# A hybrid attention and MLP layer in which the differential heads' outputs and probabilities are turned by VectorE and DRAM in place of TensorE, and their scores come one weight piece later

## The chip, the cores and the metric

One core of one Trainium2 chip runs the whole program. The metric is the device time of one execution in microseconds, the median of the runs. TensorE, VectorE, ScalarE, GpSimd and SyncE (called PE, DVE, ACT, POOL and SP in the profile) each run their own stream of instructions in order and meet at semaphores; SP issues nearly all DMAs.

## The reference, cut to what matters

The input is 256 tokens of width 2048, float32. One layer is a mixer with eight FoX heads and eight differential heads, an output projection, and a gated MLP with a causal convolution of width 3.

```python
h = rms_norm(x, norm1_g)
proj = h @ w_in                               # 2048 x 6152: q, k, v of 16 heads, 8 forget logits
# FoX head: p_f = softmax(q k' * scale + c_q - c_k, causal);  o_f = p_f @ v
#   c = cumsum(log_sigmoid(forget logits)), so every FoX head needs a row and a column of c
# differential head: two 64-wide softmaxes over a block-causal mask
a_d = p_d[:, :, 0] - lam * p_d[:, :, 1]
o_d = rms_norm(a_d @ v, diff_subln_g) * (1 - lambda_init)
x = x + concat(o_f, o_d) @ w_out
x = x + (silu(conv(h2 @ w_up)[gate]) * conv(h2 @ w_up)[val]) @ w_down
```

## The kernel before, in words

All weights are read once from DRAM in pieces of 128 partitions, by a ring of four slots (`raw`, line 305). Each piece is split into a high part (ACT, line 697, `w_hi`) and a low part (DVE, line 1138, `w_lo`), and PE multiplies it in three float32r passes. PE's order is written out by hand: the program is a row of pieces, and small attention steps are put between them.

The input projection is cut by heads into "frames" of eight pieces. Differential heads are frames 0 to 7 and their attention is numbered 1 to 8; FoX heads follow, numbered 9 to 16. While PE projects head f (counting from 0; 12 matmuls of 384 columns a piece), the other engines do the attention of head f, whose projection was frame f-1, and the end ("trail") of head f-1. Within a frame, slot b means "beside or behind piece b". On every engine the slot's own work stands in program order with the split of the piece four further on: ACT's split in slot b waits until piece b is used, and SP's load in slot b waits for DVE's split of slot b.

Before the change a differential frame goes so. PE: values of head f-1 (lines 446 to 448, which read `pT`) and transposes of q and k (line 410) after piece 2, scores (line 419, which read `qkT`) after piece 3, transposes of the output (line 465) after piece 4. ACT: `copy_p`, the copy of the turned probabilities from `p_read` to `pT` (line 774), in slot 0; `copy_qkT` (lines 737, 738) in slot 2; exponentials (line 757) in slot 3; in slot 7 the evacuation (lines 719, 722) and the guess of the norm first and the split after. DVE: row maxima (1224) and normalisation (1254) ahead of the splits of slots 3 and 4, the norm of the output (1279) in slot 2, the low part of `mixed` (1289) ahead of the split of slot 6. POOL rotates q and k (1693, 1696) once DVE has normed them, and PE's transposes wait for that.

From head 4 on the probabilities are turned without PE: DVE transposes blocks of 32x32 (`turn_p`, line 1265), SP stores them to a scratch in DRAM (line 314) in slot 3 and reads them back block by block in four DMAs (line 324) in slot 5. FoX heads from 10 on do the same in slots 6 and 7, and PE reads `p_read` itself (lines 457, 458) after piece 5 of the next frame. Heads 1 to 3, 15 and 16 use PE transposes (line 428).

In slot 6 of frame 6 SP issues `cbc` (line 355), a broadcast of all c rows to 128 partitions, and `cq` (line 356), the columns of c, an access of single elements of 4 bytes. SP's next load, slot 7 of frame 6, brings piece 7 of frame 7, which ACT splits in slot 3 of frame 7. None of this is edited by the change.

Of the kernel before, what the change touches and what calls it, by code (L numbers as in the profile page):

```python
# [13 lines left out]
P = 128  # L14
S, D, F = 256, 2048, 5504
H = 8
# [55 lines left out]
P0, P_STOP = 4, HEADS - 1  # L72
BLOCK_AT = dict(scores=5)
MOVES = {1: (0, 5), 2: (5, 16)}
DIFF_AT = dict(turn=2, scores=3)
TRAIL_AT = dict(values=2, sums=2, norm=2, turn=4, hi=5, lo=6)
CONV_TAIL = {11 + 3 * t: (FULL - 1, t, BATCH) for t in range(BATCH)} | {28 + 3 * t: (FULL, t, LAST) for t in range(LAST)}
FORGET_AT = dict(scale=0, logits=0, exp=1, log=2, turn=3)
OUT_AT = dict(turn=1, scores=2, probs=4, values=5)


def hybrid_layer_kernel(nc, xT_d, xtok_d, w0_d, win_d, wrest_d, const_d, row_d, vec_d, out_d):
    c_d = nc.dram_tensor("c_scratch", (H, S), F32, kind="Internal").ap()
    p_d = nc.dram_tensor("p_scratch", (P, SROW), F32, kind="Internal").ap()
    with ExitStack() as ctx:
# [22 lines left out]
        with ExitStack() as att:  # L108
# [40 lines left out]
            on = sa("on", S)  # L149
# [40 lines left out]
        osq_done, oturn_done, ors_done, onorm_done = sem("osq_done"), sem("oturn_done"), sem("ors_done"), sem("onorm_done")  # L190
# [48 lines left out]
        def part(t, h):  # L239

            return t.rearrange("p (k h j) -> p h k j", k=2, h=2)[:, h]

# [29 lines left out]
        def _(sp):  # L272
# [63 lines left out]
            for f in range(P0, HEADS):  # L336
                for b in range(8):
                    load_piece(8 * (f + 1) + b)
                    if H + 2 <= f < H + 6 and b == 1:
                        load_x_again(f - (H + 2))  # L340
                    if f <= H + 1 and b == 3:
                        store_p(f)
                    if f <= H + 1 and b == 5:
                        read_p(f)
                    if H + 1 < f < P_STOP and b == 6:
                        store_p(f)
                        read_p(f)
# [10 lines left out]
            sp.dma_start(conv[:], vec_d).then_inc(conv_landed, 16)  # L358
# [30 lines left out]
        def _(pe):  # L389
# [41 lines left out]
            def values(f, p, kind, first=False):  # L431
# [5 lines left out]
                if not first:  # L437
                    pe.wait_ge(mixlo_done, f - 1)
                v = [qkv[:, (p * M + m) * QKV + 2 * HD:(p * M + m + 1) * QKV] for m in range(M)]
                if kind == "fox":  # L440
                    pe.matmul(bank(B_O, 0, S), v[0], pT[:, 0:S], start=True, stop=False, skip_group_check=True)
                    pe.matmul(bank(B_O, P, P), v[1], pT[:, S:SROW], start=False, stop=True,
                              skip_group_check=True).then_inc(pv_done, 1)
                    return
# [6 lines left out]
            def block_values(f, p):  # L451

                pe.wait_ge(p_landed, f * 64 - 64 * (P0 - 1))
                pe.wait_ge(mixlo_done, f - 1)
# [5 lines left out]

            def out_transposes(f):

                pe.wait_ge(onorm_done, f)
                for m in range(M):
                    last = pe.transpose(bank(B_O, S + m * P, P), on[:, m * P:(m + 1) * P], ident)
                last.then_inc(oturn_done, 1)
# [9 lines left out]
            def attention_steps(f, p, kind, b, at):  # L476
# [7 lines left out]
                if b == at.get("values"):  # L484
                    values(f, p, kind)
# [9 lines left out]
            def frame(f, par, kind, at=None, trail=False, forget=False, spill=False):  # L495

                for b in range(8):
# [5 lines left out]
                    if trail and b == TRAIL_AT["turn"]:  # L503
                        out_transposes(f - 1)
# [52 lines left out]
            for b in range(8):  # L557
                projection(3, 1, b)
                if b == 0:
                    prob_transposes(2, "diff")  # L560
                if b == 3:
                    out_transposes(1)
                    pe.wait_ge(pT_ready, 2)
                    transposes(3, 0, "diff")
                if b == 4:
                    values(2, 1, "diff")
                    scores(3, "diff")
                if b == 6:
                    out_transposes(2)
                if b == 7:  # L570
                    prob_transposes(3, "diff")
# [10 lines left out]
            def out_piece(blk, b):  # L582

                g = 8 * blk + b
# [3 lines left out]
                for k2 in range(2):  # L588
                    kt = 2 * b + k2
                    if blk == 0 and kt >= KT - 2:  # L590
                        pe.wait_ge(mixlo_done, kt + 1)
# [9 lines left out]
            for b in range(8):  # L601
                out_piece(0, b)
                if b == 0:
                    prob_transposes(HEADS - 1, "fox")
                if b == 1:
                    values(HEADS - 1, 0, "fox")
                attention_steps(HEADS, 1, "fox", b, OUT_AT)
            for blk in range(1, OUT_BLOCKS):
                for b in range(8):
                    out_piece(blk, b)  # L610
# [80 lines left out]
        def _(act):  # L691
# [79 lines left out]
            def copy_p(f):  # L771

                act.wait_ge(p_landed, 64 * bounced(f))
                act.activation(pT[:].rearrange("p (s i t) -> p s i t", i=4, s=3),
                               p_read[:].rearrange("p (i s t) -> p s i t", i=4, s=3), ACT.Copy).then_inc(p_copied, 1)

            def mix_hi(f, kind):

                act.wait_ge(pv_done if kind == "fox" else oturn_done, f)
                if kind == "fox":  # L780
                    src, scale = bank(B_O, 0, S), 1.0
                else:
                    src, scale = bank(B_O, S, S), sg[:]
                act.activation(part(tile(mixed, f - 1, 2 * S, 2 * S), 0), by_half(src), ACT.Copy,
                               scale=scale).then_inc(mixhi_done, 1)
# [11 lines left out]
            def attention_steps(f, kind, b, at):  # L797
# [5 lines left out]
                if b == at.get("probs"):  # L803
                    copy_pT(f)
                if b == at.get("values") and kind == "fox":
                    mix_hi(f, kind)

            def trailing_steps(f, b):

                if b == TRAIL_AT["sums"]:  # L810
                    out_sums(f - 1)
                if b == TRAIL_AT["norm"]:
                    out_guess(f - 1)
                if b == TRAIL_AT["hi"]:
                    mix_hi(f - 1, "diff")
# [21 lines left out]
            def frame(f, par, kind, next_kind, at=None, trail=False, last=False, forget=False, blocks=False, spill=False):  # L837
                for b in range(8):
                    if b == 7:
                        evacuate(f * 8 + 8, par, par)  # L840
                        if next_kind == "diff" or blocks:
                            head_norm(f + 1, next_kind)
                    split_next(f, b, PW if last and b >= 4 else W1)
                    if b == 7 and next_kind == "fox" and not blocks:
                        head_norm(f + 1, next_kind)
                    if spill and b == 5:
# [8 lines left out]
                    if trail and b == 0 and f > P0:  # L855
                        copy_p(f - 1)
# [67 lines left out]
            for b in range(8):  # L924
                if b == 7:
                    evacuate(32, 1, 1)
                    head_norm(4, "diff")
                    copy_pT(3)
# [3 lines left out]
                if b == 1:  # L932
                    out_guess(1)
                    copy_pT(2, unscaled=True)
                if b == 3:
                    mix_hi(1, "diff")
                    copy_qkT(3, "diff")
                if b == 4:
                    out_sums(2)
                    out_guess(2)  # L940
                    exps(3, "diff")
                if b == 5:
                    mix_hi(2, "diff")
# [47 lines left out]
            for b in range(8):  # L991
                out_split(b + 4)
                if b == 0:
                    copy_pT(HEADS - 1)
                if b == 1:
                    mix_hi(HEADS - 1, "fox")
                attention_steps(HEADS, "fox", b, OUT_AT)
            for blk in range(1, OUT_BLOCKS):
                for b in range(8):
                    out_split(8 * blk + b + 4)  # L1000
                    x1_steps(blk - 1, b)
# [92 lines left out]
            def up_batch(nb, par, post=True, spill=True, ahead=UW, last=False):  # L1094

                for s in range(KT):
# [8 lines left out]
                    if not post:  # L1105
                        x1_steps(OUT_BLOCKS - 1, s)
# [28 lines left out]
        def _(dve):  # L1135
# [146 lines left out]
            def mix_lo(f, kind):  # L1282
# [502 lines left out]
```

## Time and profile before

| | us |
|---|---|
| median of 3 runs | 1046.55 (1044.93 to 1047.14) |
| the profiled execution's own time | 1046.72 |
| its span | 1044.9 |
| PE busy | 1038.9 (99%) |
| ACT busy | 785.3 (75%) |
| DVE busy | 744.6 (71%) |
| granted TensorE clock | 1.0 throughout |
| DMA | 217.77 MB, mean 208 GB/s |

A busy share is the union of an engine's instructions over the span. The time of one execution is 1.8 us more than the span, which begins with the first instruction of the program and ends with its last. In a timeline each row is start, duration, engine, line, operation, tiles and shapes, and in brackets the idle time before it and what ended that. Matmuls overlap, so the distance between two starts is what one costs.

### The profile page before, as it was taken

What the parts mean: (1) busy time and instruction counts of PE and PEld (TensorE: products, weight loads), DVE (VectorE), ACT (ScalarE), POOL (GpSimd) and SP (SyncE); (2) the same over time, 40 slices, a digit from 0 to 9 for tenths busy, and PEclk for the clock granted to TensorE, in tenths of its full rate; (3) what the DMA queues carried; (4) which work ended last, traced back from release to release, by engine and by line L of the source; (5) the groups of instructions that cost most, each with busy time, mean ns of one, the idle gap of its engine ahead of it and who ended that gap; (6) DMA issues with size and microseconds to landing.
All of it is one profiled execution on the core that took longest, in us unless ns stands there. A gap on an engine that the chain in (4) does not pass through costs nothing.

```text
span 1044.9 us, 16398 instructions
## 1 busy us (share of the span) xinstructions
PE 1038.9 (99%) x5327; PEld 940.0 (90%) x5327; DVE 744.6 (71%) x1237; ACT 785.3 (75%) x1376; POOL 20.9 (2%) x27
## 2 busy tenths in 40 slices
PE   9999999999999999999999999999999999999998
PEld 8999999999988888888888888888889988888887
DVE  7788878778767566577776776876867678766664
ACT  7787666788858884879788788798797778755553
POOL 0101010000000000000000000000000000000000
PEclk9999999999999999999999999999999999999999
DMA  9756676676766666666566565665655766666664
GB/s 352 235 168 191 192 229 205 212 242 229 240 212 197 204 199 204 203 214 201 189 218 197 192 223 189 201 220 183 220 182 193 232 204 202 203 202 206 205 203 145
DMA packets 75580, 217.77 MB, mean 208 GB/s; under 512 B 15864, under 2 KB 18688, under 8 KB 75392
## 3 DMA queue, kind: packets, MB, share of 16 engines
q1 hardware_dynamic: 75376, 216.79, 63.5%
q8 instruction: 35, 0.57, 0.2%
q10 hardware_dynamic: 144, 0.20, 0.1%
q14 instruction: 25, 0.20, 0.1%
HBM read 212.69 MB, written 4.27 MB: 208 GB/s over the span
## 4 chain that ended last, share of the span: by engine, by line
PE 95%; DMA 2%; DVE 1%; ACT 1%; SPq 0%; issue 0%; DVEq 0%; ACTq 0%
PE ps L621 14%; PE ps L620 14%; PE ps L622 14%; PE ps L651 7%; PE ps L649 7%; PE ps L650 7%; PE ps L397 7%; PE ps L399 7%; PE ps L398 7%; PE ps L598 3%; PE ps L596 3%; PE ps L597 3%; DMA raw<-in_win 2%; PE ps L419 1%; PE ps L410 0%; DMA p_read<-p_scratch 0%
## 5 line engine op out<-in xcount | busy, mean ns | idle before, releaser
L1138 DVE TENSOR_TENSOR w_lo<-raw,w_hi 128x1024 fp32r<-128x1024 f32 (+1 forms) x406 | 463.5, 1147 | 245.7 <-ACT w_hi L697 242.3
L697 ACT ACTIVATE w_hi<-raw 128x1024 fp32r<-128x1024 f32 (+1 forms) x406 | 398.4, 988 | 166.9 <-PE ps L651 74.8
L622 PE MATMUL ps<-w_hi,xs 128*128 128x512 f32 (+1 forms) x704 | 263.6, 374 | 0.0
L620 PE MATMUL ps<-w_hi,xs 128*128 128x512 f32 (+1 forms) x704 | 263.6, 374 | 0.0
L621 PE MATMUL ps<-w_lo,xs 128*128 128x512 f32 (+1 forms) x704 | 263.6, 374 | 0.0
L397 PE MATMUL ps<-w_hi,xs 128*128 128x384 f32 (+1 forms) x496 | 165.8, 334 | 0.5 <-DVE w_lo L1138 0.5
L399 PE MATMUL ps<-w_hi,xs 128*128 128x384 f32 (+1 forms) x496 | 161.9, 326 | 0.0
L398 PE MATMUL ps<-w_lo,xs 128*128 128x384 f32 (+1 forms) x496 | 161.9, 326 | 0.0
L620 PEld LDWEIGHTS ps<-w_hi,xs 128*128 128x128 f32 x704 | 133.2, 189 | 17.1
L621 PEld LDWEIGHTS ps<-w_lo,xs 128*128 128x128 f32 x704 | 133.2, 189 | 17.1
L622 PEld LDWEIGHTS ps<-w_hi,xs 128*128 128x128 f32 x704 | 133.2, 189 | 17.1
L650 PE MATMUL ps<-w_lo,a_s 128*128 128x512 f32 (+1 forms) x346 | 130.8, 378 | 0.0
L651 PE MATMUL ps<-w_hi,a_s 128*128 128x512 f32 (+1 forms) x346 | 130.8, 378 | 0.0
L649 PE MATMUL ps<-w_hi,a_s 128*128 128x512 f32 (+1 forms) x346 | 130.8, 378 | 0.0
L1026 ACT ACTIVATE uT<-utT 32x512 f32<-32x512 f32 (+1 forms) x176 | 109.3, 621 | 26.8 <-DVE utT L1549 22.8
L397 PEld LDWEIGHTS ps<-w_hi,xs 128*128 128x128 f32 x496 | 93.8, 189 | 3.4 <-issue 1.7
L398 PEld LDWEIGHTS ps<-w_lo,xs 128*128 128x128 f32 x496 | 93.9, 189 | 0.2
L399 PEld LDWEIGHTS ps<-w_hi,xs 128*128 128x128 f32 x496 | 93.8, 189 | 0.0
L649 PEld LDWEIGHTS ps<-w_hi,a_s 128*128 128x128 f32 x346 | 65.5, 189 | 9.1
L651 PEld LDWEIGHTS ps<-w_hi,a_s 128*128 128x128 f32 x346 | 65.5, 189 | 9.1
L650 PEld LDWEIGHTS ps<-w_lo,a_s 128*128 128x128 f32 x346 | 65.5, 189 | 9.1
L596 PE MATMUL ps<-w_hi,mixed 128*128 128x512 f32 x128 | 49.1, 383 | 0.0
(167 smaller groups left out, 938.8 us busy)
## 6 DMA issues: line engine op xcount, KB each, us to landing
raw<-in_wrest SPq DMA_DIRECT2D x278, 512.0 KB, 3.7
raw<-in_win SPq DMA_DIRECT2D x117, 384.0 KB, 3.8
raw<-in_wrest SPq DMA_DIRECT2D x16, 384.0 KB, 2.9
p_scratch<-pdT SPq DMA_DIRECT2D x11, 192.0 KB, 2.1
p_read<-p_scratch SPq DMA_DIRECT2D x44, 48.0 KB, 3.1
xtok<-in_xtok SPq DMA_DIRECT2D x4, 512.0 KB, 14.0
xv<-in_xtok SPq DMA_DIRECT2D x4, 512.0 KB, 5.9
raw_ahead<-in_w SPq DMA_DIRECT2D x5, 392.0 KB, 8.1
```

What stands on the lines that cost most here:

```text
L397: pe.matmul(o, xh, wh, start=(kt == 0), stop=False, skip_group_check=True)
L398: pe.matmul(o, xh, wl, start=False, stop=False, skip_group_check=True)
L399: last = pe.matmul(o, xl, wh, start=False, stop=(kt == KT - 1), skip_group_check=True)
L620: pe.matmul(o, xh, wh, start=(k == 0), stop=False, skip_group_check=True)
L621: pe.matmul(o, xh, wl, start=False, stop=False, skip_group_check=True)
L622: last = pe.matmul(o, xl, wh, start=False, stop=(k == KT - 1), skip_group_check=True)
L649: pe.matmul(to, ah, wh, start=start, stop=False, skip_group_check=True)
L650: pe.matmul(to, ah, wl, start=False, stop=False, skip_group_check=True)
L651: return pe.matmul(to, al, wh, start=False, stop=stop, skip_group_check=True)
L697: act.activation(slot(w_hi, s, w), slot(raw, s, w), ACT.Copy).then_inc(hi_ready, 1)
L1026: act.activation(dst, src, ACT.Copy).then_inc(u_moved, 1)
L1138: dve.tensor_tensor(slot(w_lo, s, w), slot(raw, s, w), f32(slot(w_hi, s, w)), ALU.subtract).then_inc(split_done, 1)
```

## The change

Differential outputs are no longer transposed by PE. DVE transposes 32x32 blocks of the normed output (`turn_o`), SP stores them and reads them back in four DMAs, and ACT and DVE make the two parts of `mixed` from `o_read`, three frames behind the head. `P0` goes from 4 to 2 and `P_STOP` from 15 to 16: heads 2, 3 and 15 too have their probabilities turned by DVE and DRAM. Transposes of q and k and the scores move from slots 2 and 3 to 3 and 4, in ACT and DVE with them; `copy_p` moves to slot 2, values to 4. In slot 7 ACT and DVE do the split ahead of evacuation and norm, in all frames. In the output projection piece 0 of block 1 comes ahead of piece 7 of block 0, and the steps that follow a block come one piece later. The convolution's weights are loaded in frame 10, and the reload of x starts a frame later.

```diff
-P0, P_STOP = 4, HEADS - 1
+P0, P_STOP = 2, HEADS
-DIFF_AT = dict(turn=2, scores=3)
-TRAIL_AT = dict(values=2, sums=2, norm=2, turn=4, hi=5, lo=6)
+DIFF_AT = dict(turn=3, scores=4)
+TRAIL_AT = dict(copy=2, values=4, sums=4, stats=5, guess=6)
+NORM_AT, MIX_AT = 1, 0
-FORGET_AT = dict(scale=0, logits=0, exp=1, log=2, turn=3)
-OUT_AT = dict(turn=1, scores=2, probs=4, values=5)
+FORGET_AT = dict(scale=0, logits=0, exp=1, log=2, turn=4)
+OUT_AT = dict(turn=2, scores=3, probs=5, values=6)
+LAST_BLOCK_VALUES = 4
+OUT_ORDER = [(0, b) for b in range(7)] + [(1, 0), (0, 7)] + [(1, b) for b in range(1, 8)] + [(blk, b) for blk in (2, 3) for b in range(8)]
...
+            def store_o(f):
+                sp.wait_ge(o_turned, f)
+                if f > 1:
+                    sp.wait_ge(o_landed, 64 * (f - 1))
+                sp.dma_start(o_d, onT[:]).then_inc(o_stored, 16)
+
+            def read_o(f):
+                sp.wait_ge(o_stored, 16 * f)
+                if f > 1:
+                    sp.wait_ge(dmix_lo, f - 1)
+                for j in range(4):
+                    src = o_d[:, j * 64:(j + 1) * 64].rearrange("(i r) c -> r i c", i=4)
+                    sp.dma_start(o_read[32 * j:32 * (j + 1), :].rearrange("r (i c) -> r i c", i=4), src).then_inc(o_landed, 16)
...
-                    if f <= H + 1 and b == 3:
+                    if 4 <= f <= H + 2 and b == 1:
+                        store_o(f - 2)
+                    if 4 <= f <= H + 2 and b == 3:
+                        read_o(f - 2)
+                    if 4 <= f <= H + 1 and b == 4:
                         store_p(f)
-                    if f <= H + 1 and b == 5:
+                    if 4 <= f <= H + 1 and b == 6:
                         read_p(f)
...
-                    if trail and b == TRAIL_AT["turn"]:
-                        out_transposes(f - 1)
...
             def frame(f, par, kind, next_kind, at=None, trail=False, last=False, forget=False, blocks=False, spill=False):
                 for b in range(8):
+                    split_next(f, b, PW if last and b >= 4 else W1)
                     if b == 7:
                         evacuate(f * 8 + 8, par, par)
-                        if next_kind == "diff" or blocks:
-                            head_norm(f + 1, next_kind)
-                    split_next(f, b, PW if last and b >= 4 else W1)
-                    if b == 7 and next_kind == "fox" and not blocks:
                         head_norm(f + 1, next_kind)
+                    if isinstance(f, int) and f <= H + 2 and b == MIX_AT:
+                        mix_hi(f - 3, "diff")
...
+            def turn_o(f):
+
+                dve.wait_ge(onorm_done, f)
+                if f > 1:
+                    dve.wait_ge(o_stored, 16 * (f - 1))
+                dve.transpose(onT[:].rearrange("p (j m t) -> p j m t", j=4, m=M),
+                              on[:].rearrange("p (m j t) -> p j m t", j=4, m=M)).then_inc(o_turned, 1)
...
                     before_split(f, kind, b, at, trail, p_blocks)
+                    if forget and b == FORGET_AT["log"]:
+                        forget_log()
+                    split_next(f, b, PW if last and b >= 4 else W1)
                     if b == 7:
                         norm_stats(f + 1, next_kind)
                         if p_blocks and at is BLOCK_AT:
                             turn_p(f, kind)
                         norm_apply(f + 1, 1 - p, next_kind)
-                    if forget and b == FORGET_AT["log"]:
-                        forget_log()
-                    split_next(f, b, PW if last and b >= 4 else W1)
...
+                    if isinstance(f, int) and f <= H + 2 and b == NORM_AT:
+                        norm_o(f - 2)
+                        turn_o(f - 2)
```

## Rows read from the trace of the kernel before

**Rows 1.** The page: busy time of PE, and the chain that ended last by engine.
```profile
PE 1038.9 (99%) x5327; PEld 940.0 (90%) x5327; DVE 744.6 (71%) x1237; ACT 785.3 (75%) x1376; POOL 20.9 (2%) x27
...
PE 95%; DMA 2%; DVE 1%; ACT 1%; SPq 0%; issue 0%; DVEq 0%; ACTq 0%
```
**Rows 2.** Timeline of PE (start, duration, line), around an output and a probability transpose.
```profile
75.58 0.49 PE L428 MATMUL ps<-const,pd 128*128 128x128 f32 x3
...
76.07 0.33 PE L398 MATMUL ps<-w_lo,xs 128*128 128x384 f32 x1
...
87.82 0.38 PE L465 MATMUL ps<-const,on 128*128 128x128 f32 x2
...
88.20 0.33 PE L398 MATMUL ps<-w_lo,xs 128*128 128x384 f32 x1
```
**Rows 3.** Timeline of PE at its three gaps of the diff frames.
```profile
117.71 0.33 PE L399 MATMUL ps<-w_hi,xs 128*128 128x384 f32 x1
118.34 0.49 PE L446 MATMUL ps<-qkv,pT 128*128 128x128 f32 x2 [0.30 <-ACT pT L774]
...
148.42 0.33 PE L399 MATMUL ps<-w_hi,xs 128*128 128x384 f32 x1
149.26 0.43 PE L397 MATMUL ps<-w_hi,xs 128*128 128x384 f32 x1 [0.52 <-DVE w_lo L1138]
...
154.89 0.33 PE L398 MATMUL ps<-w_lo,xs 128*128 128x384 f32 x1
155.05 0.33 PE L399 MATMUL ps<-w_hi,xs 128*128 128x384 f32 x1
156.02 0.49 PE L446 MATMUL ps<-qkv,pT 128*128 128x128 f32 x2 [0.64 <-ACT pT L774]
```
**Rows 4.** Groups by line: DVE's transposes of the probabilities.
```profile
L1265 DVE STREAM_TRANSPOSE pdT<-pd 128x384 f32<-128x384 f32 x5 | 2.9, 578 | 0.2
```
**Rows 5.** Timeline of SP's DMA queue, from slot 5 of frame 6 on.
```profile
130.13 1.80 SPq L324 DMA_DIRECT2D p_read<-p_scratch  x4
131.97 0.43 SPq L305 DMA_DIRECT2D raw<-in_win  x1
132.45 0.43 SPq L355 DMA_DIRECT2D cbc<-c_scratch  x1
132.92 0.44 SPq L356 DMA_DIRECT2D cq<-c_scratch  x1
...
135.31 5.85 SPq L305 DMA_DIRECT2D raw<-in_win  x1
```
**Rows 6.** Windows (busy us by engine, clock, DMA share, GB/s); DMA packets, 135.3 to 141.
```profile
137.00:138.50 1.50, 1.50 (x13) 1.50 (x12) 1.12 (x2) 1.17 (x3) 0.00 (x1) 1.00 1.02 179
138.50:141.00 2.50, 2.50 (x19) 1.94 (x18) 1.70 (x7) 1.23 (x8) 0.00 (x0) 1.00 0.16 24
...
DMA packets 2107, 0.99 MB, mean 173 GB/s; under 512 B 1977, under 2 KB 1977, under 8 KB 1995
```
**Rows 7.** Timeline of ACT in slots 2 and 3 of frame 7.
```profile
138.08 0.46 ACT L737 ACTIVATE qkT<-ps,qsc 128x256 f32<-128x256 f32 x1
138.44 0.37 ACT L738 ACTIVATE qkT<-ps 128x256 f32<-128x256 f32 x1
...
143.92 0.84 ACT L697 ACTIVATE w_hi<-raw 128x768 fp32r<-128x768 f32 x1 [3.93 <-DMA raw<-in_win]
```
**Rows 8.** Timeline of PE behind piece 2 of frame 7.
```profile
136.43 0.39 PE L446 MATMUL ps<-qkv,pT 128*128 128x128 f32 x2
...
137.09 0.62 PE L410 MATMUL ps<-const,qn 128*128 128x128 f32 x4
```
**Rows 9.** Timeline of POOL: the rotation of head 7.
```profile
135.96 1.05 POOL L1696 TENSOR_TENSOR qn<-rope 128x128 f32<-128x128 f32 x1
```
**Rows 10.** A FoX frame: SP's reads of the probabilities, and PE's first use.
```profile
225.96 1.76 SPq L324 DMA_DIRECT2D p_read<-p_scratch  x4
...
231.46 0.60 PE L457 MATMUL ps<-p_read,qkv 128*128 128x256 f32 x2
```

More of the change, by code:

```diff
@@ L429, in prob_transposes, with values @@
                 last.then_inc(pt_done, 1)
-            def values(f, p, kind, first=False):
+            def values(f, p, kind, first=False, o=B_O):
                 if isinstance(f, int) and P0 <= f <= H:
@@ L436, in values @@
                     pe.wait_ge(pT_ready, pe_turned(f))
-                if not first:
-                    pe.wait_ge(mixlo_done, f - 1)
+                if kind == "diff" and not first:
+                    pe.wait_ge(onorm_done, f - 1)
                 v = [qkv[:, (p * M + m) * QKV + 2 * HD:(p * M + m + 1) * QKV] for m in range(M)]
                 if kind == "fox":
-                    pe.matmul(bank(B_O, 0, S), v[0], pT[:, 0:S], start=True, stop=False, skip_group_check=True)
-                    pe.matmul(bank(B_O, P, P), v[1], pT[:, S:SROW], start=False, stop=True,
+                    pe.matmul(bank(o, 0, S), v[0], pT[:, 0:S], start=True, stop=False, skip_group_check=True)
+                    pe.matmul(bank(o, P, P), v[1], pT[:, S:SROW], start=False, stop=True,
                               skip_group_check=True).then_inc(pv_done, 1)
@@ L459, in block_values @@
                           skip_group_check=True).then_inc(pv_done, 1)
[L461 to L466, printed above, removed]
             def forget_turn():
@@ L599, in out_piece @@
                 last.then_inc(piece_used, 1)
[L601 to L610, printed above, removed]
+            for g in range(8):
+                out_piece(g)
+                attention_steps(HEADS, 1, "fox", g, OUT_AT)
+                if g == LAST_BLOCK_VALUES:
+                    block_values(HEADS - 1, 0)
+            for g in range(8, OUT_PIECES):
+                out_piece(g)
             def up_piece(nb, k, banks, w):
@@ L802, in attention_steps @@
                     exps(f, kind)
-                if b == at.get("probs"):
-                    copy_pT(f)
                 if b == at.get("values") and kind == "fox":
-                    mix_hi(f, kind)
+                    mix_hi(f, kind, B_T)
             def trailing_steps(f, b):
+                if b == TRAIL_AT["copy"]:
+                    copy_p(f - 1)
                 if b == TRAIL_AT["sums"]:
                     out_sums(f - 1)
-                if b == TRAIL_AT["norm"]:
+                if b == TRAIL_AT["guess"]:
                     out_guess(f - 1)
-                if b == TRAIL_AT["hi"]:
-                    mix_hi(f - 1, "diff")
             def forget_steps(b):
@@ L1104, in up_batch @@
                         up_steps(nb - 1, s, 1 - par)
-                    if not post:
-                        x1_steps(OUT_BLOCKS - 1, s)
+                    if not post and s < 9:
+                        x1_steps(OUT_BLOCKS - 2 + (s > 0), (s + 7) % 8)
                     if not post and s == 13:
@@ L1316, in before_split @@
                         turn_p(f, kind)
-                if trail and b == TRAIL_AT["lo"]:
-                    mix_lo(f - 1, "diff")
             def after_split(f, kind, b, at, trail=False):
@@ L1323, in after_split @@
                     forget_bias(f)
-                if trail and b == TRAIL_AT["sums"]:
+                if trail and b == TRAIL_AT["stats"]:
                     out_stats(f - 1)
-                if trail and b == TRAIL_AT["norm"]:
-                    norm_o(f - 1)
                 if b == at.get("values") and kind == "fox":
-                    mix_lo(f, kind)
+                    mix_lo(f, kind, B_T)
             def parameters():
@@ L1458, in _ @@
                     normalise(2, "diff")
+                    turn_p(2, "diff")
                     norm_stats(3, "diff")
@@ L1734, in lay_out @@
     wo = np.concatenate([wo[H:], wo[:H]]).reshape(8, 2, P, OUT_BLOCKS, HALF, 2)
-    wo = wo.transpose(3, 0, 2, 1, 5, 4).reshape(-1, PW)
+    wo = wo.transpose(3, 0, 2, 1, 5, 4)
+    wo = np.concatenate([wo[blk, b] for blk, b in OUT_ORDER]).reshape(-1, PW)
     wu = np.asarray(w_up)[0].reshape(KT, P, 2, FT * P)
```

166 lines of the change are left out of this document (97 added, 69 removed).

## The prediction, made before the changed kernel was built or run

> **What bounds the kernel now.** I read the page first, for PE's share and the chain; then PE's timeline, for what an inserted step costs and where PE stands still; then SP, DMA, ACT and POOL around the largest gap. PE is busy 1038.9 of 1044.9 us and 95% of the chain that ended last is PE [rows 1]. So only two things count: what PE no longer executes, and what PE waits for. Work on DVE, ACT, POOL and SP costs nothing unless a piece or a step of PE comes later for it.
>
> PE's price for a step is how much later the next matmul starts. With the pair at 87.82 in it, the matmul of line 398 starts at 88.20; without, L397 would start at 87.82 and L398 0.16 later, at 87.98. A pair of output transposes costs 0.22. Likewise three probability transposes cost 76.07 - 75.58 - 0.16 = 0.33 [rows 2]. Of standing still there are three places in the diff frames. Neighbouring matmuls start 0.16 apart (154.89, 155.05); the gaps are 0.63, 0.84 and 0.97, so 0.47, 0.68 and 0.81 too much, and each is followed by a first matmul some 0.1 slower (0.43 to 0.49 against 0.33 long). Together 1.96 + 0.3 = 2.2 us. The first and third wait for ACT's copy of the probabilities, the second for a low part by DVE [rows 3].
>
> **Part 1, transposes gone.** Eight output pairs (heads 1 to 8), 8 x 0.22 = 1.76; heads 2, 3 and 15 lose three probability transposes each, 3 x 0.33 = 1.0. All on PE's path: -2.75. Value matmuls, scores and q/k transposes keep their number and only change place. The replacement is one block transpose by DVE for each head, under the 0.58 that 384 columns take [rows 4], a store and four reads, and a low part in two instructions; readers are the output projection, more than six frames on for head 8, so it is off the path at a price of nothing as long as splits are not late. Bounds: nothing, and 8 x 0.6 = 4.8 if it came through whole. I take nothing: DVE is 71% busy [rows 1], every split is made four pieces ahead, and the only low part that PE missed in these frames is the one of 149.26, behind the DMA stall below [rows 3].
>
> The Trainium skill speaks against this exchange: its page "VectorE: DVE Perf Modes", section "Rules for kernel authors", says to transpose 128x128 on TensorE where PSUM will do as the destination. By that rule nothing would be won. The trace disagrees in this kernel because TensorE is the engine that sets the end and VectorE is not; the rule prices the operation by itself.
>
> **Part 2, the copy of probabilities a slot later.** The gaps at 118.34 and 156.02 are ACT waiting at the start of the frame for the last of the four reads. The change issues the reads one slot later and consumes them two slots later (slot 2), and values follow at piece 4 in place of 2. That gives one slot, over 2 us, against a delay of under 1. Both gaps go: -(0.47 + 0.81 + 0.2) = -1.5. Bounds 0 and -1.5; I take -1.5.
>
> **Part 3, the gap at 149.26.** It is the second wave of a DMA stall in frame 7, and here the change both mends and breaks. In slot 6 of frame 6 SP issues cbc and cq at 132.45 and 132.92; its next load, wanted at 135.31, takes 5.85 us to issue [rows 5]. In that window 1977 of 2107 packets are under 512 B, the single elements of cq; the DMA engines are full to 138.5 (share 1.02) and nearly idle from there to 141 (0.16) while SP still sits in the issue [rows 6]. ACT stood still for the load 3.93 us, in slot 3, until it landed at 143.9 [rows 7]. Behind it exponentials and normalisation were late, and with them the low part that PE missed at 149.26. In the new order, piece 0 of frame 8 is split ahead of exponentials, and PE will be later anyway (next). So that gap goes: -0.8.
>
> (The skill's page "DMA: Bandwidth & Descriptors", section "Rules for kernel authors", says that a non-contiguous last dimension becomes one descriptor per element. The packet count agrees; the price of it stands on the rows alone.)
>
> **Part 4, what is late next.** ACT's program in slot 3 of frame 7 is now: split of piece 7 (the load that lands late), then `copy_qkT`, which moved here from slot 2. In the trace of before that copy ran at 138.08, ahead of the blocked split [rows 7]; PE never saw the 3.93 us. Now the scores of head 7 wait for it, and PE has no work it may take past them. When does PE reach them? Its values of head 6 began at 136.43, behind three pieces, each 12 x 0.1625 = 1.95 us, so frame 7 began at 130.58; the values cost 0.66 (136.43 to 137.09) [rows 8], the four transposes 4 x 0.11 = 0.45 by the pair of [rows 2]. In the new order PE reaches the scores after five pieces, the transposes and the values: 130.58 + 9.75 + 0.45 + 0.66 = 141.44 on the old clock. When is `qkT` ready? If the load lands as before: 143.92, +0.75 until the next ACT instruction, +0.36 and +0.37 for the two copies = 145.4. Stall 4.0.
>
> But it lands later. The four reads of probabilities (1.80 us of SP) were ahead of the load of slot 6; now they are behind it, and so between that load and cbc. cbc is issued 1.6 to 1.8 us later [rows 5]. The queue was full then, so part of the delay is absorbed: the load of slot 6 goes first, and the bytes are the same. I put the shift of the landing at 0.8, between 0 (bandwidth alone sets the end) and 1.8 (issue alone). Stall 4.0 to 5.8, taken 4.8. A floor below that: the engines idled some 2.4 us (138.7 to 141.1) before SP was free [rows 6]; if that does not come again, the stall is 2.4.
>
> Frame 6 has a small sister: in slot 6 of frame 5 the reads are now ahead of the store of c and two constant loads, and the load behind them lands some 0.5 later, near where slot 3 needs it. +0.2, between 0 and 0.7.
>
> **Part 5, the frame's end.** The split of slot 7 now goes ahead of evacuation and norm, one ACT split, 0.84 [rows 7], and ACT comes there some 0.4 later, since exponentials and output sums are later in the frame. POOL's rotation of head 7 ended at 137.01 [rows 9], 0.08 before PE began the transposes at 137.09 [rows 8]. They now begin after four pieces, 7.8 us into the frame, where it was 6.5: +1.3 of room against 0.84 + 0.4 of delay. It holds with 0.1 left. I charge +0.3 for four frames; bounds 0 and 4 x 0.5 = 2.0. In FoX frames `turn_p` moves behind a split, 0.9 us later; the last read was issued at 227.7 and needed at 231.46 [rows 10], so it is still in time, and the load behind the reads loses about 0.9 of its room. Taken as nothing; bounds 0 and 6 x 0.5 = 3. In the output projection each step keeps its distance from its reader, since piece 7 of block 0 and all that waits move together: nothing, either way.
>
> **Sum.** -2.75 - 1.5 - 0.8 + 4.8 + 0.2 + 0.3 = +0.25. On the profiled execution's 1046.72 (span 1044.9 and 1.8 around it; the median of the runs is 0.17 lower) that is 1046.97, so 1046.8 for the median.
>
> **The rivals.**
> A, no new stall: if cbc and cq drain before slot 3, or the load lands by about 140, the gains stand alone: -5.05 + 0.5, 1042.0. For it: the DMA engines idled from 138.7, so the late landing is SP's issue, not bandwidth, and may depend on how the queue happens to fill. Against: 3.93 us of waiting in the very slot into which the copy moves. Between A and the forecast lies the stall of 2.4: -2.15, 1044.4.
> B, slower: the frame's end decides. If the rotation comes later than PE's fourth piece, PE waits once in each of frames 5 to 8, and in the FoX frames the late load makes piece 7 late. It decides from 0.1 us of delay more than I counted. With 0.5 in four diff frames and 0.3 in six FoX frames it gives +2.0 + 1.8 - 0.3 on top of the sum: 1050.3. For it: 0.08 us of room before. Against: room and delay both grow by nearly the same.
> C, the turn through DRAM is not off the path: 8 more stores and 32 more reads in a queue that already lands loads late. Of a frame's loads only the one behind cq was late at 149.26; 1 us more of DMA time there would come on the stall: 1047.8. Within the forecast's range.
>
> **How the numbers follow.** About 0.2% (2.1 us) is what a measurement of this kernel can tell from no change. Forecast (stall of 4 to 5.8, rest hidden), 1046.8, with its own range 1045.5 to 1048.3: chance 0.46, C included. Stall of 2.4 or none: 0.32, of it 0.28 faster by over 2.1. B: 0.22, of it 0.2 slower by over 2.1. Hence faster 0.30 (0.28, and some of the forecast's lower edge), same 0.48, slower 0.22. The range leaves a tenth out on each side: 1042.2 to 1050.
>
> **What would show it.** Right: no line 465 in the trace and no line 428 but for heads 1 and 16; no gap of PE at `copy_p`; in frame 7, after the values of head 6, a gap of 4 to 6 us before line 419 released by ACT's line of `copy_qkT`, and SP's load behind cq with an issue of 5 us or more. Wrong: that gap missing or under 3 us, gaps before line 410 released by POOL, or gaps at line 397 in FoX frames behind a DMA landing.

## The result, and the profile after

The changed kernel takes 1050.32 us (median of 16 runs, 1047.83 to 1053.12) against 1046.57 (16 runs, 1044.93 to 1048.07) for the kernel before: ratio 1.0038, 95% interval 1.0029 to 1.0047, so slower by 3.75 us. The profiled execution took 1051.29, its span 1049.5 (before: 1046.72 and 1044.9), so the traces differ by 4.6 us, a little more than the medians. The mean granted clock is below 1 in all 16 runs of the changed kernel: 0.998 in seven of them (their median is 1048.37) and 0.997 or 0.996 in nine (1051.29, and the profiled execution is one of these).

The first two lines are the page's busy time and chain by engine, which answer to [rows 1]; the third is from the view of what PE waited for (engine and line, releaser: us in total, times, longest).

```profile
PE 1038.8 (99%) x5302; PEld 941.2 (90%) x5302; DVE 751.1 (72%) x1256; ACT 784.3 (75%) x1375; POOL 18.5 (2%) x27
...
PE 79%; DVE 8%; DMA 5%; ACT 5%; issue 2%; SPq 1%; ACTq 0%; DVEq 0%
...
PE ps L465 <- ACT qkT L770: 4.9, 2, 4.1
```

PE's busy time did not fall, though PE has 25 matmuls less. The chain is no longer almost all PE, which says that one wait late in the chain reaches back through ACT, DMA and DVE. Line 465 is the scores, line 770 the second half of `copy_qkT`. Here is PE's timeline in frame 7, which answers to [rows 8]: the end of head 6's values, the scores of head 7, the matmuls behind them.

```profile
140.02 0.39 PE L494 MATMUL ps<-qkv,pT 128*128 128x128 f32 x2
144.50 1.65 PE L465 MATMUL ps<-qkT 64*128 64x128 f32 x8 [4.09 <-ACT qkT L770]
146.08 0.69 PE L443 MATMUL ps<-w_hi,xs 128*128 128x384 f32 x1
146.56 0.53 PE L444 MATMUL ps<-w_lo,xs 128*128 128x384 f32 x1
146.88 0.53 PE L445 MATMUL ps<-w_hi,xs 128*128 128x384 f32 x1
...
149.76 0.53 PE L445 MATMUL ps<-w_hi,xs 128*128 128x384 f32 x1
150.08 0.46 PE L443 MATMUL ps<-w_hi,xs 128*128 128x384 f32 x1
150.37 0.33 PE L444 MATMUL ps<-w_lo,xs 128*128 128x384 f32 x1
150.54 0.33 PE L445 MATMUL ps<-w_hi,xs 128*128 128x384 f32 x1
```

The reader is to see two losses. The first is the bracket: 4.09 us of standing still. The second has no bracket: behind it matmuls start 0.32 apart up to 150.08, and 0.16 to 0.17 apart from 150.37 on. In the windows (busy us by engine, the granted clock, DMA share, GB/s) the granted clock is 0.50 in that stretch, the level of 1.2 GHz, and 1.00, 2.4 GHz, behind it:

```profile
144.50:146.00 1.50, 1.50 (x8) 0.93 (x8) 0.30 (x1) 0.83 (x1) 0.00 (x0) 0.50 1.00 375
146.00:150.20 4.20, 4.20 (x15) 4.12 (x14) 2.44 (x13) 2.11 (x12) 0.00 (x0) 0.50 0.59 185
150.50:153.00 2.50, 2.50 (x18) 2.50 (x17) 2.19 (x5) 1.31 (x2) 0.00 (x0) 1.00 0.44 165
```

That is also why PE's busy time stayed: slow matmuls count as busy. The cause lies in SP's queue and ACT's program, the same places as [rows 5] and [rows 7]:

```profile
131.05 1.81 SPq L337 DMA_DIRECT2D p_read<-p_scratch  x4
132.90 0.43 SPq L401 DMA_DIRECT2D cbc<-c_scratch  x1
133.38 0.43 SPq L402 DMA_DIRECT2D cq<-c_scratch  x1
133.85 7.82 SPq L318 DMA_DIRECT2D raw<-in_win  x3
...
142.97 0.84 ACT L729 ACTIVATE w_hi<-raw 128x768 fp32r<-128x768 f32 x1 [6.21 <-DMA raw<-in_win]
143.72 0.46 ACT L769 ACTIVATE qkT<-ps,qsc 128x256 f32<-128x256 f32 x1
144.07 0.37 ACT L770 ACTIVATE qkT<-ps 128x256 f32<-128x256 f32 x1
```

The load behind cq landed at 142.95; the split waited 6.21 us for it, the two copies followed, and the scores started as the second ended.

Measured frame by frame (from PE's first matmul of a frame to that of the next), the two traces differ so: frames 2 to 5 together -1.6, frame 6 +0.04, frame 7 +6.03 (18.69 to 24.72), frame 8 -1.23, frames 9 and 10 -0.3, frames 11 to 15 +1.2, the output projection +0.14, start-up and frame 0 +0.4; sum +4.65. The MLP is the same within 0.03. Here frame 0 stands for the first 96 matmuls of the program; in these the projections of heads 0 and 1 alternate.

### The profile page after: what moved, and what is told of

It reads as the page before. It is cut to its first block, busy times and chain, and to the rows that moved or that the text cites. A ratio compares the mean times of both kernels' runs of the same rounds, so it can differ in the third digit from the quotient of the medians.

```text
span 1049.5 us, 16391 instructions
## 1 busy us (share of the span) xinstructions
PE 1038.8 (99%) x5302; PEld 941.2 (90%) x5302; DVE 751.1 (72%) x1256; ACT 784.3 (75%) x1375; POOL 18.5 (2%) x27
## 4 chain that ended last, share of the span: by engine, by line
PE 79%; DVE 8%; DMA 5%; ACT 5%; issue 2%; SPq 1%; ACTq 0%; DVEq 0%
PE ps L653 14%; PE ps L654 14%; PE ps L652 14%; PE ps L681 7%; PE ps L683 7%; PE ps L682 7%; DMA raw<-in_win 3%; DVE w_lo L1171 3%; PE ps L443 3%; PE ps L444 2%; PE ps L445 2%; PE ps L633 2%; PE ps L631 2%; PE ps L632 2%; ACT qkT L779 2%
```

## The experiments

Each (e1 to e12) was timed in five rounds, beside the kernel before on the same chip, whose median was 1045.66 to 1046.02. "After" is the changed kernel. Frame lengths are those of the one profiled execution. In e1, e9, e11 and e12 that execution was the longest of all, so there the trace says less of the median.

**The copy ahead of the split (e1).** In frames 6 and 7 alone:

```diff
+                    first = isinstance(f, int) and f in (6, 7) and b == at.get("turn")
+                    if first:
+                        copy_qkT(f, kind)
                     split_next(f, b, PW if last and b >= 4 else W1)
```

> The changed kernel, but in frames 6 and 7 ScalarE does the copy of q and k (copy_qkT) ahead of the split of slot 3, not behind it. Theory A (the loss is this copy queued behind a split whose load lands late, 4.2 us of standing still in frame 7 and then some 2.7 us in which TensorE runs at the lower clock, and 0.8 us in frame 6): the gap before the scores of head 7 goes and no stretch of lower clock remains; later, row maxima and normalisation still stand behind the late split on VectorE, so about 1.6 us comes back at piece 1 of frame 8. 1050.3 - 4.2 - 2.7 - 0.8 + 1.6 = 1044.2, ratio to before 0.998. Theory B (the landing of the loads, made later by the added stores and reads of the outputs, costs PE its pieces directly): the gap only moves to the low part of piece 7 of frame 7, and little is won, above 1049. Theory C (frame ends and FoX frames decide): no change, 1050.3.

Measured 1045.94, ratio 0.9996 (0.9987 to 1.0004), where theory A said 1044.2. The gap before the scores and the lower clock are gone, so the order of copy and split is what turns the late load into PE's wait. Frames 7 and 8 are still 19.12 and 20.44 long: PE now waits at the low parts, in smaller pieces, and once for POOL:

```profile
149.11 0.43 PE L443 MATMUL ps<-w_hi,xs 128*128 128x384 f32 x1 [0.59 <-DVE w_lo L1174]
152.56 0.43 PE L443 MATMUL ps<-w_hi,xs 128*128 128x384 f32 x1 [1.23 <-DVE w_lo L1174]
159.49 0.66 PE L456 MATMUL ps<-const,qn 128*128 128x128 f32 x4 [0.82 <-POOL qn L1746]
```

**PE kept running through the stall (e2).** Same stall, but PE executes 16 matmuls that nobody reads before the scores:

```diff
+                if b == at["scores"] and isinstance(f, int) and f == 7:
+                    pe.wait_ge(rowmax_done, 6)
+                    for _ in range(16):
+                        pe.matmul(bank(B_S + 1), ones[:, 0:P], ones, start=True, stop=True, skip_group_check=True)
```

> The changed kernel, with 16 bfloat16 matmuls of 512 columns on a constant put ahead of the scores of head 7, where TensorE stands still 4.2 us; their result is overwritten by the scores. They take 3.4 us at the higher clock. If the lower clock behind the gap comes from TensorE having stood still, the matmuls behind it run at 0.16 us each and not 0.32, and 2.7 us are won while the wait for the copy stays: 1047.6, ratio 1.001. If the lower clock comes from something else that happens at that time (the burst of loads, or the slow matmuls are a result of waiting for operands), nothing is won: 1050.3, ratio 1.0036.

Measured 1048.08, ratio 1.0018 (1.0009 to 1.0027), against 1.0038 for after.

```profile
140.08 0.39 PE L494 MATMUL ps<-qkv,pT 128*128 128x128 f32 x2
140.30 3.66 PE L525 MATMUL ps<-const-bfloat16-1.0 128*128 128x512 bf16 x16
144.74 0.93 PE L465 MATMUL ps<-qkT 64*128 64x128 f32 x8 [0.77 <-ACT qkT L774]
145.59 0.43 PE L443 MATMUL ps<-w_hi,xs 128*128 128x384 f32 x1
145.86 0.33 PE L444 MATMUL ps<-w_lo,xs 128*128 128x384 f32 x1
...
144.00:150.00 6.00, 5.26 (x35) 4.93 (x36) 3.65 (x15) 3.92 (x17) 0.00 (x0) 1.00 0.78 254
```

The scores start as late as in after (144.74, there 144.50), but the next projection matmul comes 0.85 behind them where it was 1.58, the granted clock stays 1.00, and frame 7 is 22.10 long for 24.72. The mean granted clock is 1.0 in all 11 runs. So the lower clock is a loss of its own, 2.6 us in the trace and 2.1 in the ratios, and it comes from PE standing still.

**What holds the load up: cq as rows (e3).** cq read as 128 rows of 64 bytes, 128 pieces in place of 2048 (its values then stand in other places):

```diff
-sp.dma_start(cq[:], c_d.rearrange("h (m p) -> p (h m)", p=P), allow_slow_non_contiguous=True
-             ).then_inc(cq_landed, 16)
+sp.dma_start(cq[:], c_d.rearrange("h s -> (h s)").rearrange("(p c) -> p c", p=P)).then_inc(cq_landed, 16)
```

> The changed kernel, with the load of cq (2048 single elements) replaced by one of the same bytes in 128 rows of 64 bytes; the columns of c for the FoX heads are then in another order, which is what this kernel computes differently. If the single elements hold up SyncE's next load (6.5 us in its issue), that load is issued and lands at least 3 us earlier, the gaps before the scores of head 7 and the lower clock go: 1050.3 - 6.9 = 1043.4, ratio 0.997. If the 1 MB broadcast cbc ahead of it is what fills the queue, the load still takes over 4 us to issue and the gap stays over 2 us: 1048 or more.

Measured 1045.62 (1043.01 to 1048.90), ratio 0.9998 (0.9986 to 1.0009), between the two expected values. In the trace the lower clock and half of the stall are gone. Not so in every execution: the mean granted clock is 1.0 in seven runs (median 1043.96) and 0.998 in five (median 1047.02), which is a large part of their scatter.

```profile
133.05 0.43 SPq L402 DMA_DIRECT2D cq<-c_scratch  x1
133.52 0.43 SPq L318 DMA_DIRECT2D raw<-in_win  x1
...
142.14 0.93 PE L464 MATMUL ps<-qkT 64*128 64x128 f32 x8 [2.06 <-ACT qkT L769]
```

The load behind cq was issued in 0.43 us; in the trace of after the same view shows 6.51:

```profile
133.85 6.51 SPq L318 DMA_DIRECT2D raw<-in_win  x1
```

It landed at 140.58, 2.4 earlier, and the gap of 2.06 brought no lower clock in this execution. So the single elements hold the load up. The rest of its lateness stands beside cbc, 1 MB, which landed at 139.58; that cbc causes it is not shown, since no run changes cbc alone.

**The FoX frames with the old frame's end (e4).** On ACT:

```diff
+                    if b == 7 and blocks:
+                        evacuate(f * 8 + 8, par, par)
+                        head_norm(f + 1, next_kind)
                     split_next(f, b, PW if last and b >= 4 else W1)
```

and the same on DVE for frames 10 to 15.

> The changed kernel with the old order at the end of the FoX frames 10 to 15 alone: evacuation, norm and the turn of the probabilities ahead of the split of slot 7. Theory A': the later turn holds up SyncE's loads, and this is the 0.76 us of frame 12 and the 0.28 us of frame 14: frames 10 to 15 come back to 16.91 each, 1050.3 - 1.1 = 1049.2, ratio 1.0025. Theory C (the frame's end is the main loss): 1046.5 or less. If the FoX gaps have nothing to do with it: 1050.3.

Measured 1048.96, ratio 1.0030 (1.0019 to 1.0042). Frames 12 and 14 are 17.02 and 16.91 here for 17.67 and 17.19, as expected, but the interval overlaps that of after. The last experiment takes this up again. The trace also holds the stall once more, 4.20 long, and here the clock was low only from 145.5 on and for a shorter time:

```profile
144.50:145.40 0.90, 0.90 (x9) 0.57 (x9) 0.29 (x1) 0.67 (x1) 0.00 (x0) 1.00 0.65 259
145.50:148.80 3.30, 3.30 (x11) 3.30 (x12) 2.23 (x10) 1.43 (x7) 0.00 (x0) 0.50 0.54 162
149.00:152.00 3.00, 3.00 (x20) 3.00 (x19) 2.65 (x8) 2.19 (x8) 0.00 (x0) 1.00 0.39 135
```

Frame 7 is 23.71 long, 1.0 less than in the trace of after. The price of the clock is thus no fixed number.

**cbc and cq in eight parts (e5)**, a head's 128 KB and 256 elements in each of eight slots, from slot 7 of frame 6 on:

```diff
+                    if 8 * 6 + 7 <= 8 * f + b < 8 * 6 + 15:
+                        h = 8 * f + b - (8 * 6 + 7)
+                        sp.dma_start(cbc[:, h * S:(h + 1) * S], c_d.rearrange("h s -> (h s)")[h * S:(h + 1) * S].partition_broadcast(P)
+                                     ).then_inc(cbc_landed, 16)
+                        sp.dma_start(cq[:, h * M:(h + 1) * M], c_d.rearrange("h (m p) -> h p m", p=P)[h],
+                                     allow_slow_non_contiguous=True).then_inc(cq_landed, 16)
```

> The changed kernel with cbc and cq cut by heads into eight loads each, one pair in each slot from slot 7 of frame 6 to slot 6 of frame 7, 128 KB and 256 elements a pair, each behind the slot's load of a piece. Theory A (one load that lands late, behind one block of cbc and cq, makes the whole loss): no load is held up, frame 7 takes 17.8 us as frames 5 and 8 do, and the lower clock goes with the gap: 1050.3 - 6.9 = 1043.4, ratio 0.997. The cell of cq alone, with cbc whole, left a gap of 2.1 us; if the bytes themselves are too many for frame 7, gaps of over 1 us stay spread over frame 7 and its time is over 19: 1045 or more.

Measured 1050.47, ratio 1.0040 (1.0026 to 1.0054): a miss. The stall moved one frame on, with its lower clock:

```profile
162.69 1.66 PE L468 MATMUL ps<-qkT 64*128 64x128 f32 x8 [4.24 <-ACT qkT L773]
...
162.70:168.50 5.80, 5.80 (x23) 5.15 (x24) 3.15 (x15) 3.19 (x14) 0.00 (x0) 0.55 0.46 133
```

A part of only 256 elements, issued at 154.63, landed at 160.18, and the 384 KB load issued behind it at 155.11 landed at 161.14. The other seven parts landed 3.7 to 5.3 us after their issue. The cut did not take the stall away, but the run does not say whether the elements or the eight parts of cbc, 128 KB each, make the late load: both were cut at once.

**The same parts in the kernel before (e6).**

> The kernel before with the same cut of cbc and cq. Its gaps at 149.26 and 156.02 (0.78 and 0.88 us) come from the same late load, so both go: 1046.6 - 1.7 = 1044.9, ratio 0.998. If the second gap is only the read of the probabilities coming late by itself, as at 118.34, it stays: 1045.8.

Measured 1047.57, ratio 1.0019 (1.0010 to 1.0028): a miss too. The gap at 149.26 of [rows 3] is gone, that at 156 stays (here 155.13, 0.52 of idle time), and the kernel is slower.

**The old slots (e7).** After, with transposes at slot 2, scores at 3 and the frame's end in the old order, the rest as changed:

```diff
-DIFF_AT = dict(turn=3, scores=4)
+DIFF_AT = dict(turn=2, scores=3)
```

> The changed kernel with transposes of q and k, scores and what follows them back in slots 2 and 3, and the old order at the end of every frame; outputs and probabilities still go through DRAM and values stay at piece 4. The copy of q and k is then ahead of the late load again. Theory A: the gap of 4.2 us and the lower clock go, 1050.3 - 6.9 - 0.8; but transposes now come 0.66 us earlier in the frame than before, since the values no longer stand ahead of them, and the rotation on GpSimd ended only 0.1 us before them: 0.5 us of waiting in each of five frames, + 2.5: 1045.1, ratio 0.9985. If the rotation doesn't hold them up: 1042.6. If the traffic of the outputs through DRAM is what costs (theory B): 1048 or more.

Measured 1045.92, ratio 1.0000 (0.9991 to 1.0009). No stall of 4 us: without the moved slots this DMA does not reach PE in that way. Instead PE waited five times for POOL:

```profile
101.26 0.66 PE L456 MATMUL ps<-const,qn 128*128 128x128 f32 x4 [0.47 <-POOL qn L1743]
...
PE ps L456 <- POOL qn L1743: 2.6, 5, 0.7
```

**The remedies together (e8)**: copy first in frames 4 to 9, parts, old end in the FoX frames.

> The changed kernel with three repairs: the copy of q and k ahead of the split of slot 3 in frames 4 to 9, cbc and cq cut by heads into eight loads each, and the old order at the end of the FoX frames. Theory A: frames 4 to 9 take 17.8 us, the FoX frames 16.91: 1050.3 - 6.9 - 0.8 - 1.1 = 1041.5, ratio 0.995. If transposes and stores of the output had a price beside these, it stays above 1043.

Measured 1046.28, ratio 0.9998 (0.9988 to 1.0009): a miss. Frames 6 and 7 are 17.76 as expected, but frame 9 is 19.46, with a wait for a low part and one for `on`, and frame 12 is 18.08, with the other wait for a low part. Why they came is not shown.

```profile
PE ps L446 <- DVE w_lo L1180: 1.5, 2, 0.8
PE ps L495 <- DVE on L1321: 0.9, 1, 0.9
```

**No DMA of single elements (e9).** After, with cq made by PE and DVE from `cT`, which is in SBUF, and cbc issued one slot later, behind that slot's load:

```diff
-                    if f == 6 and b == 6:
+                    if f == 6 and b == 7:
                         sp.dma_start(cbc[:], ...).then_inc(cbc_landed, 16)
-                        sp.dma_start(cq[:], ...).then_inc(cq_landed, 16)
+                    if isinstance(f, int) and f == 6 and b == 4:
+                        for m in range(M):
+                            last = pe.transpose(bank(B_T, m * H, H), cT[:, m * P:(m + 1) * P], ident[0:H, 0:H])
```

> The kernel after, with the gate columns cq made on TensorE (two transposes of cT in slot 4 of frame 6, copied by VectorE in slot 5) in place of the DMA of single elements, and the load of cbc issued in slot 7 of frame 6 behind that slot's raw load instead of in slot 6. If the DMA of single elements is what brings the split of slot 3 late, the gap of 4.1 us before the scores of head 7 in frame 7 and the stretch at the lower granted clock behind it are gone: frame 7 some 18.0 instead of 24.7, time 1043.5, ratio 0.997. The gap of 0.8 us in frame 6 stays. If instead the 1 MB of cbc (or the DMA engines) hold the loads late wherever it stands, a gap of 2 us or more stays in frame 7 or 8: 1047 or more.

Measured 1044.17 (1041.70 to 1045.70), ratio 0.9981 (0.9973 to 0.9990): faster than before by 2.0 us, where 3.1 were expected.

```profile
133.88 0.43 SPq L319 DMA_DIRECT2D raw<-in_win  x1
134.35 0.43 SPq L402 DMA_DIRECT2D cbc<-c_scratch  x1
...
139.35 0.84 ACT L734 ACTIVATE w_hi<-raw 128x768 fp32r<-128x768 f32 x1 [1.44 <-DMA raw<-in_win]
140.10 0.46 ACT L774 ACTIVATE qkT<-ps,qsc 128x256 f32<-128x256 f32 x1
...
141.46 0.93 PE L466 MATMUL ps<-qkT 64*128 64x128 f32 x8
```

No bracket stands behind the scores: ACT's wait for the load fell from 6.21 to 1.44. Frame 7 is 17.76. The edit does two things at once, and which part the later cbc has in it is not separated. The wait of frame 6 is still there, as the expectation says:

```profile
123.48 0.93 PE L466 MATMUL ps<-qkT 64*128 64x128 f32 x8 [0.64 <-ACT qkT L775]
```

**The best version (e10)**: that, with the copy ahead of the split in frames 4 to 7 and the old end in the FoX frames.

> e9 together with the copy of head b's queries and keys ahead of the split in frames 4 to 7, and the frame's end of the kernel before in the FoX frames (10 to 15), whose old order gave back 1.0 us in the trace of e4. If the losses add, the 0.8 us gap of frame 6 goes too and frames 12 and 14 are 16.9: 1041.6, ratio 0.9955. If the copy ahead of the split only turns one gap into several small ones at the low parts, as in the frames of e1 and e8, it is no better than e9: 1043.5.

Measured 1042.36 (1041.72 to 1043.61), ratio 0.9966 (0.9953 to 0.9979), faster than both kernels. Frames 4 to 8 are 17.76 to 17.98 long, and PE is 99% of the chain, where it was 95% in the kernel before:

```profile
PE 99%; DMA 0%; DVE 0%; ACT 0%; issue 0%; DVEq 0%
```

**The same edit of cq and cbc in the kernel before (e11).**

> The kernel before with the same edit (cq by TensorE, no DMA of single elements, cbc in slot 7 of frame 6). Its frame 7 had gaps of 0.8 and 1.1 us behind the late load of slot 2 and after it. If the DMA of single elements makes them: 1044.9, ratio 0.9985, so that the change itself is worth about -1.5 us with that DMA out of the way in both. If frame 7's gaps stay, they are the copy's and the low part's own: 1046.5.

Measured 1045.75, ratio 0.9998 (0.9989 to 1.0007): frames 7 and 8 fell by 1.7 (18.01 each), but the median did not follow; in its trace frame 12 and the output projection took 2.3 more. The median lies between the two expected values, and the interval leaves room for up to 1.2 us of gain. So the DMA cost the kernel before little, and with it out of the way in both the change is worth 1044.17 - 1045.75 = -1.6 as an estimate: the two intervals, 0.9973 to 0.9990 and 0.9989 to 1.0007, just touch.

**The FoX frames again (e12)**: e9 with the edit of e4.

> e9 with the frame's end of the kernel before in the FoX frames alone (copy after the split, as in the kernel after). If the new frame's end is what costs in frames 12 and 14, they come down from 17.9 and 17.2 in the trace of e9 to 17.0 and 16.9 and the median goes from 1044.2 to 1043.0 (ratio 0.9972), and the copy ahead of the split in frames 4 to 7 is worth the remaining 0.6 of e10. If those frames vary by themselves from run to run, as frame 12 of e11 (18.3 with the old end) suggests, it stays at 1044.2 (0.9983), and e10's gain of 1.8 over e9 is the copy's.

Measured 1043.58, ratio 0.9980 (0.9971 to 0.9989), between the two expected values. In its trace frame 12 took 18.08 and frame 14 17.65 although the old end is in. So the reading of the fourth experiment falls: frame 12 varies from execution to execution with either end, by 1.4 us with the old one (16.91 in before, 18.28 in e11) and 1.0 with the new one (16.91 in e1, 17.94 in e9). What of e10's further 1.8 us is the copy ahead of the split and what is scatter is not settled: e9's, e10's and e12's intervals overlap.

## Why the prediction was wrong, point by point

**Part 1** held. Line 474, probabilities turned by PE, is left for heads 1 and 16, no output transposes are in the trace, and DVE's replacement takes 0.445 for a head, hidden. **Part 2** held: PE waits for no `pT` in the diff frames. **Part 3** held: the gap at 149.26 has no successor. Where no stall hits, a diff frame takes 17.76 (frame 8 of after, frame 7 of e9). With 6.96 (24.72 - 17.76) taken off frame 7 and 0.84 off frame 6, frames 2 to 10 are 4.87 shorter than before; the forecast for parts 1 to 3 was 5.05, of it 4.7 in these frames, since head 15's transposes stood in the output projection (from 289.8 on in the trace of before).

**Part 4 is the step that failed, and in what it left out.** Its stall was foretold right in place and releaser, and nearly in size: 4.8 taken, 4.0 to 5.8 as bounds, 4.3 measured (22.10 - 17.76, frame 7 of e2). The 0.8 put down for the later landing was too much: the load landed 13.56 us into frame 7, before 13.33. But the sum put down the standing still and nothing for what follows it. The missing term is PE's lower clock, +2.6 us in the trace and 2.1 in the ratios: shown by e2, where the stall stays and the term goes. With it the sum is 1048.9 to 1049.4 for the median, and the measured 1050.32 would have been foretold as slower. A row to warn of it was not in the trace of before, where the clock is granted in full throughout and no gap of the diff frames is over 1 us [rows 3]. The Trainium skill's page "TensorE: Matmul & The Clock Gate", section "What's actually happening", says that the array's clock is halved or not by how busy the engine has been of late; the traces agree (granted 0.50 behind gaps of 4.1 and 4.2 us, 1.00 behind gaps of 1.2 and 2.1 in the traces of e1 and e3), and that rule should have stood beside a stall forecast at 4 to 5.8 us, as a rival at the least.

Two smaller sizes in it were off. Frame 6's sister was 0.84, not 0.2, over its bound of 0.7: the load behind the small DMAs landed at 121.02, 10.2 us into the frame, before 9.1, so 1.2 later where 0.5 was taken. Rival A's ground, that the late landing is SP's issue and not bandwidth, was right for most of it (e3, e9), but it did not go away by itself.

**Part 5.** For the diff frames the charge of 0.3 was not needed: PE waited nowhere for POOL, and e7 shows the other side of the margin, 0.5 to 0.7 in each of five frames once the transposes stand a slot earlier. FoX frames and output projection were taken as nothing and show +1.3 in the trace of after, though head 15's 0.33 should have come off. By e12 and by the same frames of e11 most of that may be scatter between executions, not the change: the output projection takes 85.61 in the traces of e2, e3, e7, e9, e10 and e12, 0.4 less than before. Its cause stays open.

**The rivals.** B's number, 1050.3, was the measured one, but its mechanism did not occur; hitting by another road is no evidence for it. C did not occur as put: the stores and reads of the outputs do not stand ahead of either late load, and e7, which keeps them, has no stall behind a load.

In numbers, profile against profile: +0.25 forecast, +4.65 measured. The difference of 4.4 is, to rounding, +2.6 clock, +0.6 frame 6, +1.2 FoX frames, +0.5 output projection (0.33 of gain not seen, and 0.14), +0.4 start-up, less 0.5 (stall), 0.3 (part 5) and 0.2 of more gain in frames 2 to 10.

## What to carry to other kernels

Price a stall of TensorE twice: its length, and the lower clock that can follow it; here 4.1 to 4.2 us of standing still made a frame 6.0 to 7.0 us longer. In a kernel without such gaps no row warns of the second. Before a step is moved behind an instruction that waits for a load, look for the latest load of the whole run in that place: an engine that waits off the path, as ACT did for 3.93 us before, becomes the path by a change of order alone. And where a small DMA of single elements holds up a queue, make the values another way; here cutting it in parts, together with the broadcast beside it, won nothing.

## What the runs showed of the hardware that was not expected

After a standstill of 4.1 us TensorE ran at 1.2 GHz for some 5.7 us of full work (144.5 to 150.2), and e5 shows the same behind 4.2. Behind the same stall in e4 it was 3.3 us (145.5 to 148.8), and PE's first 0.9 us of work behind the gap still had 1.00. Gaps of 2.1 (e3) and 1.2 (e1) did not bring it in their traces; but five of the 12 runs of e3 and one of the 12 of e9 have a mean granted clock of 0.998, as the runs of after have. How long PE stood still in those is not known.

A DMA of single elements holds up what is issued behind it on the same queue. Its own landing says little of that: 2048 elements took 7.9 us to land and the same bytes as 128 rows 6.8 (e3), both behind a cbc of 7.6 and 7.0. The difference is in the next load: 6.51 us of issue behind the elements, 0.43 behind the rows. The Trainium skill's page "Perfetto Trace Analysis", section "DMA Instruction — HWDGE (DVE, Sync)", says that the descriptor generator is held for one instruction until its descriptors are made; SP's issues of 5.85 us in [rows 5] and 6.51 in after agree.

At the start of the program the speed of TensorE differs between executions. In the first 3.5 us of full work (6.0 to 9.5) the best version (e10) executed 13 matmuls and the kernel before 20, in that order:

```profile
6.00:9.50 3.50, 3.50 (x13) 3.50 (x12) 2.35 (x6) 2.37 (x6) 0.00 (x0) 1.00 1.03 387
```

```profile
6.00:9.50 3.50, 3.15 (x20) 2.84 (x19) 1.98 (x5) 2.15 (x5) 0.00 (x0) 1.00 1.02 375
```

The view gives a granted clock of 1.00 for both, but the matmuls of e10 speak against it. They start 0.33 apart up to 9.08 (two in 0.65) and 0.16 apart from 9.72 on, the two spacings that frame 7 of after has at 0.50 and at 1.00:

```profile
7.77 0.86 PE L570 MATMUL ps<-w_hi,xs 128*128 128x392 f32 x2
8.43 0.86 PE L573 MATMUL ps<-w_lo,xs 128*128 128x392 f32 x2
9.08 0.80 PE L567 MATMUL ps<-w_hi,xs 128*128 128x384 f32 x2
9.72 0.49 PE L570 MATMUL ps<-w_hi,xs 128*128 128x384 f32 x2
10.04 0.49 PE L573 MATMUL ps<-w_lo,xs 128*128 128x384 f32 x2
```

So the clock of 1.00 that the view gives for the first microseconds of a trace is not to be relied on; the distance between matmuls is. Frame 0 is 18.20 long in e10 and 16.67 in the kernel before, though both execute the same there: differences under 1.5 us between single traces of this kernel have to be read frame by frame.
